# Two blocks with three mixtures of experts on one core: routing of all groups at once, rounding ahead, overflow slots behind the first gathers

## Chip, cores, metric

The kernel runs on one core of one Trainium2 chip. The metric is device microseconds of one execution; lower is better. All data are 32-bit floats. On TensorE "f32" products are full ones; operands named `..._parts` hold values rounded to the short form fp32r, and a high and a low part together stand for the full value.

## What is computed

Two blocks over 256 tokens of width 1,024. The first has two layers (an attention mixer and a MoE each), the second one layer (state-space mixer, attention and a wider MoE). What the change touches is the MoE's choice of experts, the same in all three:

```python
def hier_moe(h, wg, bg, we, be, w_gate, w_up, w_down):
    ...
    gl = (t @ wg + bg).astype(jnp.float32)
    gp = jax.nn.softmax(gl, axis=-1)
    _, gsel = lax.top_k(gl, 1)
    g_oh = jax.nn.one_hot(gsel[:, 0], MOE_GROUPS, dtype=jnp.float32)
    gw = jnp.sum(gp * g_oh, axis=-1, keepdims=True)
    el = (t @ we + be).astype(jnp.float32).reshape(n, MOE_GROUPS, MOE_PER_GROUP)
    el_g = jnp.sum(el * g_oh[:, :, None], axis=1)
    tv, ti = lax.top_k(el_g, MOE_TOPK)
    tw = jax.nn.softmax(tv, axis=-1)
    w_grp = jnp.sum(jax.nn.one_hot(ti, MOE_PER_GROUP, dtype=jnp.float32) * tw[..., None], axis=1)
    comb = ((g_oh * gw)[:, :, None] * w_grp[:, None, :]).reshape(n, MOE_EXPERTS)
    a = jax.nn.silu(jnp.einsum('td,edf->tef', t, w_gate)) * jnp.einsum('td,edf->tef', t, w_up)
    y = jnp.einsum('tef,efd->td', a * comb[:, :, None].astype(a.dtype), w_down)
```

There are 16 experts; the hidden width is 256 in the two MoEs of the first block and 512 in that of the second.

## The kernel before

Everything is written out by hand as one instruction stream per engine, with semaphores. Tokens lie on the 128 partitions in two tiles (`tt` 0 and 1). Weights come through a ring of six slots of 2,048 KB each, filled by SyncE's queue in a fixed order (`PHASES`); the load of tile n waits until `tile_used` says that tile n - 6 has been read. TensorE's stream raises `tile_used` when it has done the last product on a tile.

The three MoEs are called `moe0`, `moe1` (function `small_experts`) and `moe2` (function `wide_experts`). Each is built the same way:

1. The second normalisation's result (`pb`, columns 0 to 1,023) is transposed by TensorE (`token_transposes`, L2164), evacuated with the modulation by ScalarE and VectorE (`trans_out`, L937 and L1303), and multiplied by the router's 20 columns (`thin_products`, L2312; `thin_folded`, L2321). ScalarE also rounds the same rows into high parts (`rounded_pairs`, L994), and GpSimd forms the low parts from them (`low_pairs`, L790).
2. VectorE's `routing` adds the bias (L1481), finds the best group, then that group's best and second expert (`first_of_max` three times, one after the other), and writes `chosen` (L1500). TensorE's `places` (L2335 to L2337) counts the tokens of each expert; VectorE turns that into `place` and into the selection matrices `wide_sel` (L1514), 64 slots for each expert, 8 experts a half.
3. TensorE gathers: `gather(half, c)` multiplies column block c of the rows by the selection (L2375 in the small ones, L2572 in the wide one). `inputs` multiplies the gathered rows by the gate and up weights (L2405, L2627), `down` by the down weights (L2454, L2701), and the result is scattered back.
4. Between the router and the gathers TensorE works on weight tiles of the modulation (`mod_tile`, L2205: four of them in `moe0` and `moe1`, two in `moe2`); ScalarE copies the raw result (L914), and `mod_turn` (L2217) transposes it.

`moe2` has extra slots for experts that more than 64 tokens chose: two experts of each half. VectorE's `more_slots` finds them (L1682 to L1712), writes the selection `more_sel` (L1706, semaphore `more_selected`) and the experts' numbers. GpSimd reads the numbers and copies ("picks", L826) those experts' weights from each pair of ring slots into `picked`; TensorE gathers their rows (`gather_more`, L2582) and multiplies them (L2643). Since the picks read the ring, a pair's slots may be released only after `picked`.

Steps on VectorE that depend on each other are joined by `step`, which waits for the instruction's own semaphore.

## Time and profile before

| what | us |
|---|---|
| three runs | 1330.98, 1336.9, 1338.33 |
| median of them | 1336.9 |
| span of the profiled execution | 1338.1 |

The profiled execution has no time of its own beside its span; the span lies between the second and third of the runs. "Span" is from the first to the last instruction. TensorE is busy 92% of it, the DMA queue of the weights 71.8%, VectorE 33%, ScalarE 20%, GpSimd 9%. In times below, us are counted from the span's start. PEclk is the TensorE clock that was granted, as a share of 2.4 GHz; its lower level is 0.50, 1.2 GHz. The first small MoE runs from about 203 to 341, the second from 565 to 704, the large one from 1058 to 1328.

### The profile page before, as it was taken

What the parts mean: (1) busy time and instruction counts of PE and PEld (TensorE: products, weight loads), DVE (VectorE), ACT (ScalarE), POOL (GpSimd) and SP (SyncE); (2) the same over time, 40 slices, a digit from 0 to 9 for tenths busy, and PEclk for the clock granted to TensorE, in tenths of its full rate; (3) what the DMA queues carried; (4) which work ended last, traced back from release to release, by engine and by line L of the source; (5) the groups of instructions that cost most, each with busy time, mean ns of one, the idle gap of its engine ahead of it and who ended that gap; (6) DMA issues with size and microseconds to landing.
All of it is one profiled execution on the core that took longest, in us unless ns stands there. A gap on an engine that the chain in (4) does not pass through costs nothing.

```text
span 1338.1 us, 17906 instructions
## 1 busy us (share of the span) xinstructions
PE 1237.0 (92%) x7488; PEld 654.8 (49%) x7488; DVE 438.6 (33%) x1143; ACT 265.7 (20%) x622; POOL 115.2 (9%) x202
## 2 busy tenths in 40 slices
PE   4999989999899899999996999999999599999996
PEld 4445745434445665554345855555544443332333
DVE  1102644113313574431144743331123730201133
ACT  0102511121101364111121221113320211120110
POOL 1010010000111000100001000000000222223221
PEclk9899999999899799999997999999999699999999
DMA  9956958999943565399997433294326479999994
GB/s 354 376 171 201 387 213 305 387 387 387 344 144 130 211 230 188 142 364 387 386 387 254 171 126 104 86 382 147 110 85 237 161 290 377 381 378 399 383 384 154
DMA packets 173803, 357.43 MB, mean 267 GB/s; under 512 B 15845, under 2 KB 20502, under 8 KB 173718
## 3 DMA queue, kind: packets, MB, share of 16 engines
q1 hardware_dynamic: 159904, 352.33, 71.8%
q10 hardware_dynamic: 13814, 3.87, 1.3%
q8 instruction: 64, 1.05, 0.3%
q14 instruction: 21, 0.17, 0.0%
HBM read 355.14 MB, written 1.05 MB: 266 GB/s over the span
## 4 chain that ended last, share of the span: by engine, by line
PE 81%; DMA 8%; DVE 5%; ACT 2%; issue 2%; SPq 1%; POOL 0%; DVEq 0%; ACTq 0%
PE bank L2187 19%; PE bank L2627 9%; PE bank L2405 7%; PE bank L2205 5%; PE bank L2923 4%; PE bank L2280 4%; DMA ring<-in_w_down 3%; PE bank L2454 3%; PE bank L2983 3%; DMA ring<-in_moe_w_down 3%; PE bank L2375 3%; PE bank L2701 2%; PE bank L2474 2%; PE bank L2272 2%; DMA ring<-in_ada_w 1%
## 5 line engine op out<-in xcount | busy, mean ns | idle before, releaser
L2187 PE MATMUL bank<-ring,hT 128*128 128x512 f32 x384 | 170.3, 603 | 2.6 <-ACT hT L937 2.4
L2627 PE MATMUL bank<-ring,A 128*64 128x512 f32 x512 | 118.1, 609 | 1.6 <-DVE pb L1784 1.6
L2187 PEld LDWEIGHTS bank<-ring,hT 128*128 128x128 f32 x384 | 73.4, 194 | 91.8 <-issue 91.8
L2405 PE MATMUL bank<-ring,A 128*64 128x512 f32 x512 | 116.0, 598 | 0.0
L2187 PE MATMUL bank<-ring,OT 128*128 128x512 f32 x224 | 97.2, 593 | 1.3 <-ACT OT L1260 0.8
L2205 PE MATMUL bank<-ring,cact 128*32 128x128 f32 x2304 | 84.5, 303 | 9.1 <-DMA ring<-in_ada_w 6.8
L778 POOL TENSOR_TENSOR rstd<-rstd,nhalf 128x1 f32<-128x1 f32 x20 | 15.9, 796 | 797.3 <-DVE rstd L1329 797.3
L2205 PEld LDWEIGHTS bank<-ring,cact 128*32 128x32 f32 x2304 | 70.3, 122 | 22.9 <-issue 15.1
L2627 PEld LDWEIGHTS bank<-ring,A 128*64 128x64 f32 x512 | 35.5, 139 | 74.2 <-issue 73.4
L2187 PEld LDWEIGHTS bank<-ring,OT 128*128 128x128 f32 x224 | 42.2, 190 | 53.5 <-issue 52.5
L2405 PEld LDWEIGHTS bank<-ring,A 128*64 128x64 f32 x512 | 34.2, 136 | 65.3 <-issue 64.2
L2454 PE MATMUL bank<-ring,pb 128*64 128x512 f32 x256 | 57.7, 597 | 2.1 <-DMA ring<-in_moe_w_down 2.1
L2280 PE MATMUL bank<-ring,hT 128*128 128x512 f32 x128 | 55.8, 594 | 0.0
L2923 PE MATMUL bank<-hT,ring 128*128 128x256 f32 x256 | 55.8, 380 | 0.0
L2923 PEld LDWEIGHTS bank<-hT,ring 128*128 128x128 f32 x256 | 48.5, 190 | 6.7 <-issue 0.2
L2983 PE MATMUL bank<-ring,hT 128*128 128x512 f32 x96 | 42.6, 593 | 0.0
L2164 PE MATMUL bank<-ident,pb 128*128 128x128 f32 x128 | 21.7, 331 | 22.0 <-issue 16.4
L2280 PEld LDWEIGHTS bank<-ring,hT 128*128 128x128 f32 x128 | 24.2, 190 | 29.1 <-issue 29.0
L937 ACT ACTIVATE hT<-bank,modc 128x128 f32<-128x128 f32 x48 | 18.0, 459 | 102.8 <-PE bank L2164 101.4
L2454 PEld LDWEIGHTS bank<-ring,pb 128*64 128x64 f32 x256 | 17.6, 136 | 37.4 <-issue 28.5
L567 DVE COPY PT<-bank 128x384 f32<-128x384 f32 (+1 forms) x34 | 17.8, 522 | 52.9 <-PE bank L2297 50.6
L1580 DVE TENSOR_TENSOR A_parts<-bank,OT_parts 128x512 fp32r<-128x512 f32 x32 | 21.6, 690 | 37.9 <-ACT OT_parts L1044 37.8
(491 smaller groups left out, 1701.4 us busy)
## 6 DMA issues: line engine op xcount, KB each, us to landing
...
```

Source lines behind the costliest of these rows:

```text
L2187: ins = mm(B[2 * (m % 2) + tt][:], lhs[:, c, tt * P:(tt + 1) * P], w[:, c, :], start=c == 0, stop=c == C - 1)
L2205: ins = mm(B[MOD_RAW_BANK[G]][32 * q:32 * (q + 1), k * P:(k + 1) * P], cact[:, c0 + c:c0 + c + 1].broadcast_to([P, 32]), w[:, c, q * P:(q ...
L2272: ins = mm(dst, lhs, rhs, start=start, stop=stop)
L2280: ins = mm(B[2 + tt][:], hT[:, c, tt * P:(tt + 1) * P], w[:, c, :], start=c == 0, stop=c == C - 1)
L2375: ins = mm(bank[:], part[:, tt, c * P:(c + 1) * P], wide_sel[:, tt, 512 * half:512 * (half + 1)], start=tt + l == 0, stop=tt + l == 2)
L2405: ins = mm(B[b][64 * odd:64 * (odd + 1), :], wide_h[c][:, slot:slot + 64], w[:, 2 * pair + odd, :, r, :], start=c == 0, stop=c == C - 1)
L2454: ins = mm(B[r][64 * b:64 * (b + 1), :], hidT_small[half][k][:, slot:slot + 64], w[:, 2 * r + b, :], start=k == 0, stop=k == 1)
L2474: ins = mm(B[5 - j + tt][:], wT_small[NR * half + r][:, P * tt:P * (tt + 1)], part[r], start=half + r + l == 0, stop=half == 1 and r + l = ...
L2627: ins = mm(B[b][64 * odd:64 * (odd + 1), :], wide_h[c][:, slot:slot + 64], w[:, 2 * pair + odd, r, :], start=c == 0, stop=c == C - 1)
L2701: ins = mm(B[r][64 * b:64 * (b + 1), :], hidT_wide[half][k][:, slot:slot + 64], w[:, 2 * r + b, :], start=k == 0, stop=k == 3)
L2923: ins = mm(B[2 * (m % 2) + a // 2][:, (a % 2) * T:(a % 2 + 1) * T], w[:, c, a * P:(a + 1) * P], hT[:, c, :], start=c == 0, stop=c == C - 1)
L2983: ins = mm(B[4 + u % 2][:], hT[:, c, (u % 2) * P:(u % 2 + 1) * P], w[:, c, :], start=c == 0, stop=c == C - 1)
```

## The change

1. `routing`: `first_of_max` now works on the group logits and on all four groups' expert logits at once (a tile of 5 x 4 in place of 1 x 4, in the new buffer `rk`). The second `first_of_max` finds each group's second expert. The best group's rows are picked out only at the end, in `chosen` and in the weights. One of three `first_of_max` goes.
2. ScalarE rounds the second token tile (`rounded_pairs(..., 1, ...)`) before it evacuates that tile's transposition, and in `moe2` GpSimd waits for the second normalised tile before it forms the low parts of the first.
3. In the small MoEs `places` stands behind the first modulation tile and the first gather behind the second.
4. In `moe2` the selection of the second half, `select("moe2", 1)`, and the overflow slots (`more_experts`, `more_slots`) are written behind the first gathers' evacuations; TensorE's wait for `more_selected` moves from ahead of all `inputs` to the first `gather_more`.
5. In `moe2`, for the first pair of weight tiles, the wait for `picked` moves behind the main products, and both slots are released together after the overflow products.

```diff
@@ low_pairs (GpSimd) @@
+            if i == 2:
+                pool.wait_ge(s["xn_ready"], MOE["moe2"]["before"] + TT)
             for tt in range(TT):
@@ scalar, for moe0 (the same for moe1 and, with x_high, moe2) @@
         rounded_pairs("moe0", 0, x_high_small)
+        rounded_pairs("moe0", 1, x_high_small)
         trans_out("h1", modulated(0, 3), [1])
         thin_copied("h1")
-        rounded_pairs("moe0", 1, x_high_small)
         pairs_copied("moe0")
@@ vector @@
+        maxima = rk[:].rearrange("p t r e -> p t (r e)")[:, :, 52:61]
+        group_hot, top_hot, second_hot = rk[:, :, 0, :], rk[:, :, 1:5, :], rk[:, :, 9:13, :]
+
+        def select(name, half):
+
+            n, (e0, e1) = MOE[name]["slots"], (8 * half, 8 * half + 8)
+            for tt in range(TT):
+                ins = v.tensor_tensor(wide_sel[:, tt, n * e0:n * e1].rearrange("p (e k) -> p e k", k=n),
+                                      bc(place[:, tt, e0:e1], 2, [P, e1 - e0, n]),
+                                      bc(slot_no[:, 0:n], 1, [P, e1 - e0, n]), ALU.is_equal)
+            ins.then_inc(s["selected"], 1)
...
-            first_of_max(goh, gl, mg, 1)
-
-            prod = rt[:, :, 9:13, :]
-            step(v.tensor_tensor(prod, prod, bc(rt[:, :, 2, :], 3, [P, TT, 4, 4]), ALU.mult))
-            el = rt[:, :, 3:4, :]
-            step(v.tensor_reduce(rt[:, :, 3, :], prod.rearrange("p t g e -> p t e g"), AX.X, ALU.add))
-            first_of_max(rt[:, :, 4:5, :], el, m1, 1)
+            best = rt[:, :, 13:15, :].rearrange("p t r e -> p t (r e)")
+            first_of_max(rk[:, :, 0:5, :], lg, maxima[:, :, 0:5], 5, best[:, :, 0:5])
+            others = rk[:, :, 5:9, :]
             for tt in range(TT):
-                ins = v.scalar_tensor_tensor(rt[:, tt, 6, :], rt[:, tt, 4, :], NEG, rt[:, tt, 3, :], ALU.mult, ALU.add)
+                ins = v.scalar_tensor_tensor(others[:, tt], top_hot[:, tt], NEG, lg[:, tt, 1:5, :], ALU.mult, ALU.add)
             step(ins)
-            first_of_max(rt[:, :, 5:6, :], rt[:, :, 6:7, :], m2, 1)
-            step(v.tensor_tensor(rt[:, :, 6, :], rt[:, :, 4, :], rt[:, :, 5, :], ALU.add))
+            first_of_max(second_hot, others, maxima[:, :, 5:9], 4, best[:, :, 0:4])
+            step(v.tensor_tensor(others, top_hot, second_hot, ALU.add))
...
+            select(name, 0)
             if name == "moe2":
                 return
+            select(name, 1)
@@ wide_experts, vector @@
+            more_experts()
             gathered(0, 1)
             mod_columns(9)
+            more_slots()
             for c in range(1, C, 2):
...
+                if c == 3:
+                    select("moe2", 1)
...
         routing("moe2")
-        more_slots()
         wide_experts(gate2)
@@ small_experts, tensor @@
-            for k in range(3):
+            mod_tile(G, 0)
+            places(i)
+            mod_tile(G, 1)
+            gather(0, 0)
+            for k in range(2, 4):
                 mod_tile(G, k)
-            places(i)
-            mod_tile(G, 3)
-            gather(0, 0)
             mod_turn(G)
@@ wide_experts, tensor @@
-                if c:
+                if c == 0:
+                    pe.wait_ge(s["more_selected"], 2)
+                else:
...
-                if quad:
+                ahead = quad and n > n0 + 1
+                if ahead:
                     pe.wait_ge(s["picked"], (n - n0) // 2 + 1)
...
                 if quad:
+                    if not ahead:
+                        pe.wait_ge(s["picked"], 1)
...
-                    ins.then_inc(tile_used, 1)
+                    ins.then_inc(tile_used, 1 if ahead else 2)
...
-            pe.wait_ge(s["more_selected"], 2)
```

TensorE in `moe0`, from the fold of the router's columns to the first product on expert weights. `cact` is the condition, `Pm` the raw modulation, `pb_parts` the high parts and the selection, `OT_parts` the low parts. Before:

```order
L2205 MATMUL bank<-ring,cact 32x128 x96
L2335 MATMUL bank<-chosen,tri_one 128x32
L2336 MATMUL bank<-chosen,tri_one 128x32
L2337 MATMUL bank<-chosen,tri_one 128x16
L2205 MATMUL bank<-ring,cact 32x128 x32
L2375 MATMUL bank<-pb_parts 128x512
L2375 MATMUL bank<-pb_parts,OT_parts 128x512
L2375 MATMUL bank<-pb_parts 128x512
L2375 MATMUL bank<-pb_parts,OT_parts 128x512
L2217 MATMUL bank<-ident,Pm 128x128 x4
L2375 MATMUL bank<-pb_parts 128x512
L2375 MATMUL bank<-pb_parts,OT_parts 128x512
```

After:

```order
L2220 MATMUL bank<-ring,cact 32x128 x32
L2350 MATMUL bank<-chosen,tri_one 128x32
L2351 MATMUL bank<-chosen,tri_one 128x32
L2352 MATMUL bank<-chosen,tri_one 128x16
L2220 MATMUL bank<-ring,cact 32x128 x32
L2390 MATMUL bank<-pb_parts 128x512
L2390 MATMUL bank<-pb_parts,OT_parts 128x512
L2390 MATMUL bank<-pb_parts 128x512
L2390 MATMUL bank<-pb_parts,OT_parts 128x512
L2220 MATMUL bank<-ring,cact 32x128 x64
L2232 MATMUL bank<-ident,Pm 128x128 x4
L2390 MATMUL bank<-pb_parts 128x512
```

The three counting products moved up by two modulation tiles, and the first gather (four products of 128x512) by two tiles as well; the turn (`ident,Pm`) now follows the last modulation tile directly.

VectorE in `moe2`, from the selection to the second gather's evacuation. `dts` holds the overflow's working values, `cs` a product with `place`, `wr` the modulation columns by pairs, `A` the gathered rows. Before, from the selection on (its four instructions in one row), and the last rows ahead of the evacuation:

```order
L1514 TENSOR_TENSOR pb_parts<-place,slot_no 128x512 x4
L1682 COPY dts<-bank 128x16
L1683 TENSOR_SCALAR dts<-dts 128x16
L1684 MEMSET dts 128x96
L1685 SCALAR_TENSOR_TENSOR dts<-dts,slot_no 128x16
L1686 TENSOR_REDUCE dts<-dts 128x2
L1687 TENSOR_TENSOR dts<-dts 128x2x8
```

```order
L1706 TENSOR_TENSOR pb_parts<-dts,slot_no 128x128 x2
L1709 TENSOR_TENSOR dts<-dts,slot_no 128x64
L1710 TENSOR_REDUCE dts<-dts 128x4
L1711 TENSOR_SCALAR expert_id<-dts 128x2
L1712 TENSOR_SCALAR expert_id<-dts 128x2
L1746 TENSOR_SCALAR A<-bank,wr 128x512
L1353 TENSOR_TENSOR modc<-bank,cols 128x8
L1356 TENSOR_SCALAR modc<-modc 128x8
L1357 MEMSET mark 128x1
```

After (lines of the changed kernel), the selection (two instructions) and then the last rows of `more_experts` and what follows:

```order
L1520 TENSOR_TENSOR place<-bank,chosen 128x32
L1483 TENSOR_TENSOR pb_parts<-place,slot_no 128x512 x2
L1690 COPY dts<-bank 128x16
L1691 TENSOR_SCALAR dts<-dts 128x16
L1692 MEMSET dts 128x96
L1693 SCALAR_TENSOR_TENSOR dts<-dts,slot_no 128x16
L1694 TENSOR_REDUCE dts<-dts 128x2
```

```order
L1702 TENSOR_REDUCE dts<-dts 128x2
L1703 TENSOR_TENSOR dts<-dts 128x2x8
L1758 TENSOR_SCALAR A<-bank,wr 128x512
L1356 TENSOR_TENSOR modc<-bank,cols 128x8
L1359 TENSOR_SCALAR modc<-modc 128x8
L1360 MEMSET mark 128x1
L1709 TENSOR_TENSOR cs<-place,dts 128x64 x2
L1711 TENSOR_REDUCE dts<-cs 128x8
L1712 TENSOR_SCALAR dts<-dts 128x8
L1715 SCALAR_TENSOR_TENSOR dts<-dts 128x2 x2
L1718 TENSOR_TENSOR pb_parts<-dts,slot_no 128x128 x2
L1721 TENSOR_TENSOR dts<-dts,slot_no 128x64
```

The evacuation `A<-bank,wr` and the three rows of the modulation columns behind it moved from behind the last of the overflow's rows into their middle, ahead of the product with `place`.

ScalarE in `moe0`, at the second token tile. `hT` is the transposed and modulated input, `pb_parts` the high parts, `PT` the router's sums. Before:

```order
L994 CAST pb_parts<-pb 128x1024
L937 ACTIVATE hT<-bank,modc 128x128 x4
L908 COPY PT<-bank 128x256
L994 CAST pb_parts<-pb 128x1024
L999 COPY wr<-bank 128x16
```

After:

```order
L997 CAST pb_parts<-pb 128x1024 x2
L940 ACTIVATE hT<-bank,modc 128x128 x4
L911 COPY PT<-bank 128x256
L1002 COPY wr<-bank 128x16
```

The second rounding (`CAST`) moved from behind the copy of the router's sums to ahead of the four activations.

## Rows read from the trace of the kernel before

**Rows 1.** The page: span, and the chain that ended last, by engine.
```profile
span 1338.1 us, 17906 instructions
...
PE 81%; DMA 8%; DVE 5%; ACT 2%; issue 2%; SPq 1%; POOL 0%; DVEq 0%; ACTq 0%
```

**Rows 2.** Windows, `moe0`: busy us by engine, granted clock, DMA share, GB/s.
```profile
235.00:240.00 5.00, 5.00 (x24) 2.44 (x24) 0.81 (x1) 0.78 (x1) 0.00 (x0) 1.00 1.05 387
```

**Rows 3.** Timeline of `moe0`: start, us, engine, line, operation, count, [idle before].
```profile
201.44 1.13 ACT L994 CAST pb_parts<-pb 128x1024 fp32r<-128x1024 f32 x1
...
203.11 6.58 PE L2205 MATMUL bank<-ring,cact 128*32 128x128 f32 x192
...
212.97 0.59 ACT L914 COPY Pm<-bank 128x512 f32<-128x512 f32 x1 [9.57 <-PE bank L2205]
...
213.89 0.60 PE L2217 MATMUL bank<-ident,Pm 128*128 128x128 f32 x4
```

**Rows 4.** Waits of TensorE on weight loads: us in total, times, longest us.
```profile
PE bank L2454 <- DMA ring<-in_moe_w_down: 2.1, 2, 1.5
...
PE bank L2701 <- DMA ring<-in_w_down: 2.7, 4, 1.1
```

**Rows 5.** Timeline of TensorE in `moe2`.
```profile
1051.27 1.97 PE L2164 MATMUL bank<-ident,pb 128*128 128x128 f32 x8 [1.11 <-DVE pb L1337]
...
1058.26 5.62 PE L2205 MATMUL bank<-ring,cact 128*32 128x128 f32 x128
...
1066.33 0.50 PE L2572 MATMUL bank<-pb_parts 128*128 128x512 f32 x1 [1.68 <-DVE pb_parts L1514]
...
1071.87 0.50 PE L2572 MATMUL bank<-pb_parts 128*128 128x512 f32 x1 [3.20 <-DVE pb_parts L1706]
...
1073.39 4.88 PE L2627 MATMUL bank<-ring,A 128*64 128x512 f32 x16
...
1080.16 3.65 PE L2627 MATMUL bank<-ring,A 128*64 128x512 f32 x16
```

**Rows 6.** Timeline of VectorE in `moe2`.
```profile
1042.06 0.81 DVE L1337 TENSOR_SCALAR pb<-x,mv,rstd 128x1024 f32<-128x1024 f32 x1
...
1048.86 2.35 DVE L1337 TENSOR_SCALAR pb<-x,mv,rstd 128x1024 f32<-128x1024 f32 x1
...
1057.41 0.26 DVE L1481 TENSOR_TENSOR rt<-bank,br 128x20 f32<-128x20 f32 x2 [2.77 <-PE bank L2321]
...
1057.91 1.88 DVE L1467 TENSOR_TENSOR rt<-rt 128x8 f32<-128x8 f32 x1
...
1063.36 0.19 DVE L1500 TENSOR_TENSOR chosen<-rt 128x32 f32<-128x32 f32 x1
...
1067.39 0.17 DVE L1682 COPY dts<-bank 128x16 f32<-128x16 f32 x1
...
1070.13 0.36 DVE L1697 TENSOR_TENSOR cs<-place,dts 128x64 f32<-128x64 f32 x2
...
1071.32 0.49 DVE L1706 TENSOR_TENSOR pb_parts<-dts,slot_no 128x128 fp32r<-128x128 f32 x2
```

**Rows 7.** Timeline of GpSimd in `moe2`.
```profile
1048.26 2.40 POOL L790 TENSOR_TENSOR A_parts<-pb,pb_parts 128x1024 fp32r<-128x1024 f32 x1
...
1057.35 2.41 POOL L790 TENSOR_TENSOR A_parts<-pb,pb_parts 128x1024 fp32r<-128x1024 f32 x1 [6.69 <-ACT pb_parts L994]
...
1075.19 0.61 POOL L826 COPY PT<-ring 128x512 f32 x1 [15.43 <-issue]
```

**Rows 8.** Windows, `moe2`: busy us by engine, granted clock, DMA share, GB/s.
```profile
1058.00:1064.00 6.00, 6.00 (x137) 5.51 (x136) 5.25 (x24) 0.22 (x2) 1.77 (x1) 0.65 0.20 37
...
1070.00:1076.00 6.00, 4.13 (x12) 1.58 (x14) 3.25 (x17) 0.78 (x1) 0.81 (x2) 0.72 0.69 278
...
1076.00:1082.00 6.00, 6.00 (x34) 2.94 (x32) 1.95 (x8) 0.46 (x1) 1.48 (x3) 1.00 0.00 0
...
1310.00:1316.00 6.00, 6.00 (x34) 1.76 (x32) 0.00 (x0) 0.00 (x0) 1.17 (x2) 1.00 0.88 328
```

53 lines of the change are left out of this document (27 added, 26 removed).

## Prediction

> **What bounds the kernel now.** I read the page first: the span is 1338.1 us and the chain that ended last is 81% TensorE, 8% DMA and only 5% VectorE [rows 1]. So a cheaper routing on VectorE is worth something only where TensorE waits for it. Next I read the DMA rate in windows. Inside the first small mixture of experts (MoE) the DMA engines are busy all the time and move 387 GB/s [rows 2]. A weight tile of 2,048 KB (2.097 MB) takes 2.097/387 = 5.4 us at that rate. Then TensorE's waits: in the two small MoEs it waits twice for a down-projection tile, 2.1 us in all, the longest 1.5, so the other 0.6; in the large one it waits 2.7 us in four pieces for such tiles [rows 4]. Each small MoE thus has a DMA stream that starts when TensorE releases the first modulation tile (by the code, a tile's load waits for `tile_used`) and does not pause; what TensorE does a little later in front of that wait is swallowed by it. Last I read the timelines around the three routings, where the edits are.
>
> **The small MoEs (moe0; moe1 has the same order).** *Routing.* TensorE does not wait for VectorE here: its three modulation tiles run from 203.11 for 6.58 us [rows 3], and the choice of experts is made beside them. The chain from the sum of logits to `chosen` has 22 waited steps before and 14 after; in the large MoE it reads from 1057.41 to 1063.55, 6.1 us, of which 1.88 - 0.17 = 1.7 us is one stalled comparison [rows 6]. A step costs about 0.2 us, and the new ones (40 elements in place of 8) should cost the same, since the sum over 20 elements twice takes 0.26 us. After: 14 x 0.21 = 3.0 us. The gain is 3.1 us on VectorE, worth nothing here as long as the modulation tiles cover it.
>
> *TensorE's new order.* `places` and the first gather now stand between modulation tiles. The same products run, but the first gather no longer lies between the last modulation tile and `mod_turn`, where it hid ScalarE's copy of the raw modulation (0.59 us, from 212.97; the turn followed at 213.89) [rows 3]. TensorE will stand still for that copy and two handovers: +0.8 us. The slots of the second to fourth modulation tile come free 0.8 to 1.8 us later, but the slot of the first comes free when it did, and one queued tile feeds the DMA engines for 5.4 us, so the stream does not pause. The 0.8 us meets the later wait: hidden in moe0 (1.5 us of wait), all but 0.2 us hidden in moe1 (0.6 us). If that cover were gone it would be +1.6 us.
>
> *Rounding ahead.* ScalarE's second rounding takes 1.13 us and began at 201.44 [rows 3]; now it stands before the four activations that empty the second tile's transposition bank, and they slip by up to about 0.5 us in moe0. The same rows are also waited for from VectorE, which leaves +0.2 us on the path to the router and so on the start of the DMA stream. In moe1 nearly nothing. Bounds 0 and +0.5 for each; I take +0.2 together. What it buys is that GpSimd's second `low_pairs` ends before the routing's first comparison; in moe2 the two began within 0.6 us of each other [rows 6, 7], which is the stall. Sum of both small MoEs: +0.4 us, bounds 0 and +2.6.
>
> **The large MoE (moe2), where the gain is.** Step by step from [rows 5] to [rows 7]:
> 1. GpSimd waits for the second normalised tile before it forms the low parts. Before, its first `low_pairs` (1048.26, 2.40 us) overlapped VectorE's normalisation, which took 2.35 us against 0.81 us for the same form at 1042.06. Now that ends 1.5 us earlier. TensorE had waited 1.11 us for it (transpositions at 1051.27), so the path gains 1.1 us; the other 0.4 us goes to the thin products in front. The Trainium skill, "SBUF — State Buffer", section "Who interferes with whom", says that VectorE and GpSimd share a port pair as an exclusive lock, so that the loser waits for the whole instruction. The two long rows agree; by the rule the reordering would be free of such stalls, as the sum has it.
> 2. Router, modulation tiles (1058.26 for 5.62 us), `places` and the first half of the selection keep their length: `chosen` at about 1059.4 is no longer close to the tiles' end at 1062.8, but it was already covered. So the faster routing is again worth 0, and everything up to the end of `mod_turn` moves by 1.1 us: the first gather from 1066.33 to 1065.2, the turn's end from 1071.87 - 3.20 = 1068.67 to 1067.6.
> 3. The wait of 3.20 us for the overflow slots (`more_selected`) goes. Gather 2 follows at once. It took 1071.87 to 1073.39, 1.5 us; the first two and the short turn took 2.34 us together, so a gather about 1.0 us. Behind the wait the granted clock was the lower of its two levels, 1.2 GHz, for part of the time (0.72 of 2.4 GHz in 1070 to 1076, 1.00 in the next window) [rows 8]. The 16 products of the first weight tile took 4.88 us there against 3.65 us for the next. I take the full clock for both, since the pause that came ahead of the slow rows is gone: first weight tile 1068.6 to 1072.2, second (after the same 1.9 us of gathers) 1074.1 instead of 1080.16. That is 6.1 us: 1.1 + 3.2 + 0.5 + 1.2, rounded.
> 4. What is late next. VectorE: half a selection (1.25 us of 2.50) is left out, so `more_experts` runs from 1067.39 - 1.25 - 1.1 = 1065.0 for 2.7 us (1070.13 - 1067.39). Gather 1's evacuation (0.81 us) ends at 1068.6, and is needed for the second half of the first tile, 1070.4. The modulation columns (0.6 us) and `more_slots` (1070.13 to 1071.81, 1.7 us) end at 1070.9. The overflow gather needs them at 1072.2: 1.3 us to spare. GpSimd began its picks 1075.19 - 1071.81 = 3.4 us after that point, so at 1074.3, and four of 0.61 us end at 1076.7. The changed code waits for them only behind the main products, at 1077.7: 1.0 us to spare. Without that move TensorE would wait 2.6 us.
> 5. DMA. The price of step 4's move is that the first slot is released not by the first product of the second tile but after all of its overflow products, at about 1078.8 (1.0 us for eight, an estimate from the gather's four). Before, it came at 1080.2; only 1.4 us are gained for the first load, about 6 us for the second. The queue was empty then (0 GB/s in 1076 to 1082) and stops at about 1315 (328 GB/s in 1310 to 1316) [rows 8]. The 42 tiles behind the first six need 42 x 5.4 = 228 us; they had 1315 - 1081 = 234, so DMA idled some 6 us in between, mostly in the first pass, where two tiles take TensorE 3.65 x 2 + 1.9 + 2 = 11.2 us and DMA 10.8. That slack lets the loads catch up to TensorE's 6.1 us, nearly. The end of the stage hangs on the last loads [rows 4], so it is their gain that counts: at least 1.4, at most 6.1. I take 5.6, since the later passes leave DMA little idle time to recover the rest.
> 6. The second half of the selection (1.25 us) runs behind the second overflow column block, when VectorE is idle, over 30 us ahead of the gathers that read it: 0. The overlap of GpSimd's picks with `route_weights` may stretch a few VectorE steps; slot sums need them much later: 0.
>
> **Sum.** -5.6 + 0.4 = -5.2 us on the profiled span: 1338.1 to 1332.9. The three runs have their median at 1336.9, 1.2 below the span, so 1331.7 (-0.39%). A change under 0.5% (6.7 us) is about what a measurement of this kernel cannot tell from none.
>
> **Rivals.**
> - *Forecast, 0.58:* 1329.5 to 1333.
> - *DMA takes most of it, 0.20.* If loads in the middle passes run slower than 387 GB/s, or never idle, the later first release rules: gain 1.4 to 3.8, minus 0.4 to 2.6. For it: the small MoEs run at full rate throughout, and the large one nearly does. Against it: 6 us of slack. Time 1334.5.
> - *More is gained, 0.17.* The granted clock was 0.65 in 1058 to 1064, so at 1.2 GHz through most of the two modulation tiles (5.62 us for 128 products, against 6.58 for 192 in moe0) [rows 3, 5, 8]. If less idle time raises it up to 3 us sooner, another 1 to 2 us come, and moe0's and moe1's +0.4 may be 0. With 6.1 from step 3: -8, so 1329. The Trainium skill, "TensorE: Matmul & The Clock Gate", section "The HAM clock gate", says that the slow level is the default and activity lifts it; the slow rows behind the pause agree.
> - *Slower, 0.05.* TensorE's clock falls back in the idle time ahead of the first gather (1.68 us) and stays down through pass 0. Each weight tile then costs up to 3.65 us more; 1.5 tiles eat the gain, and from 3.4 tiles the kernel is slower by over 0.5%. With four, 1331.7 + 14.6 = 1346. Against it: that same idle time did not lower it before.
> - *The change does nothing:* if `more_selected` is as late as TensorE's need by 3 us more than reckoned; it has 1.3 us to spare. Within the second case.
>
> **Range and chances.** The cases from DMA-bound to more gained hold 0.95. Cutting half of each outer tail, and with runs of the kernel before 7 us apart, 1328.3 to 1335.8. Faster by over 0.5% (below 1330.2): 0.17 plus a sixth of the forecast case, 0.27. Slower by over 0.5%: 0.05. Within: 0.68.
>
> **What would show it.** Right: `low_pairs` three times without a long VectorE row beside it; TensorE's wait for `more_selected` gone and the first two weight tiles both at 3.65 us; a pause of 0.7 us before `mod_turn` in moe0 and moe1; the wait for the down tile there shorter by 0.8; the second weight tile of moe2 6 us nearer to the router. Wrong: TensorE waiting for picks or for the overflow slots, more wait for down tiles in moe2 than 2.7 us, or a small MoE that is longer by over 1 us.

## The result, and the profile after

The changed kernel took 1324.12 us, the median of 4 runs (1321.49 to 1324.61), beside 1336.95 us for the kernel before in the same session (4 runs, 1330.98 to 1338.33). The ratio is 0.9913 with a 95% interval of 0.9885 to 0.9941: faster by 12.8 us, where 5.2 were forecast, and below the range of 1328.3 to 1335.8. The profiled execution fell from 1338.1 to 1321.8 us, by 16.3.

The page of the changed kernel: its span, the granted TensorE clock in 40 slices, and the chain that ended last by engine.

```profile
span 1321.8 us, 17890 instructions
...
PEclk8999999999899899999997999999999699999998
...
PE 84%; DVE 5%; DMA 5%; ACT 3%; issue 2%; SPq 1%; POOL 0%; DVEq 0%; ACTq 0%
```

In the chain that ended last TensorE is 84% in place of 81%, and DMA fell from 8% to 5% [rows 1]. Next TensorE's timeline in the large MoE of the changed kernel.

```profile
1034.94 1.33 PE L2179 MATMUL bank<-ident,pb 128*128 128x128 f32 x5 [4.23 <-DVE pb L1340]
...
1042.10 1.97 PE L2179 MATMUL bank<-ident,pb 128*128 128x128 f32 x8
...
1049.09 5.96 PE L2220 MATMUL bank<-ring,cact 128*32 128x128 f32 x128
...
1057.50 0.50 PE L2588 MATMUL bank<-pb_parts 128*128 128x512 f32 x1 [1.68 <-DVE pb_parts L1483]
...
1059.63 0.50 PE L2588 MATMUL bank<-pb_parts 128*128 128x512 f32 x1
...
1060.75 3.65 PE L2646 MATMUL bank<-ring,A 128*64 128x512 f32 x16
1064.34 0.33 PE L2600 MATMUL bank<-pb_parts 128*128 128x128 f32 x1
...
1066.30 3.65 PE L2646 MATMUL bank<-ring,A 128*64 128x512 f32 x16
1069.88 0.62 PE L2664 MATMUL bank<-PT,cols 128*32 128x512 f32 x1
```

The waits of 1.11 us ahead of the second row and of 3.20 us ahead of the second gather (now at 1059.63) [rows 5] are gone, and both weight tiles take 3.65 us. From the first row, the transposition with which the part begins, to the second weight tile it took 31.4 us. In the kernel before that transposition stands here:

```profile
1042.92 1.97 PE L2164 MATMUL bank<-ident,pb 128*128 128x128 f32 x8 [3.88 <-DVE pb L1337]
```

So before it took 1080.16 - 1042.92 = 37.2 us. VectorE's timeline of the changed kernel beside it:

```profile
1040.88 0.80 DVE L1340 TENSOR_SCALAR pb<-x,mv,rstd 128x1024 f32<-128x1024 f32 x1
...
1048.55 0.20 DVE L1469 TENSOR_REDUCE rk<-rt 128x10 f32<-128x40 f32 x1
1048.78 0.20 DVE L1470 TENSOR_TENSOR rk<-rt,rk 128x40 f32<-128x40 f32 x1
...
1051.35 0.19 DVE L1506 TENSOR_TENSOR chosen<-rk 128x32 f32<-128x32 f32 x1
...
1062.42 0.49 DVE L1718 TENSOR_TENSOR pb_parts<-dts,slot_no 128x128 fp32r<-128x128 f32 x2
```

And GpSimd's:

```profile
1041.76 4.77 POOL L793 TENSOR_TENSOR A_parts<-pb,pb_parts 128x1024 fp32r<-128x1024 f32 x2 [1.45 <-DVE pb L1340]
1066.30 0.61 POOL L829 COPY PT<-ring 128x512 f32 x1 [19.76 <-issue]
1066.85 1.17 POOL L829 COPY tmp<-ring 128x512 f32 x2
1067.96 0.61 POOL L829 COPY gate<-ring 128x512 f32 x1
```

The normalisation takes 0.80 us, no step of the choice is stalled, and GpSimd has done both low parts (1041.76 + 4.77 = 1046.5) before the choice starts at 1048.55. The overflow slots are ready at 1062.9, 1.4 us ahead of the gather that wants them at 1064.34. The picks end at 1068.6 and are wanted at 1069.88. In `moe0` the timeline shows the new order's two small waits:

```profile
202.44 1.95 PE L2220 MATMUL bank<-ring,cact 128*32 128x128 f32 x64
205.33 0.41 PE L2350 MATMUL bank<-chosen,tri_one 128*128 128x32 f32 x2 [0.93 <-DVE chosen L1506]
...
214.31 0.55 PE L2232 MATMUL bank<-ident,Pm 128*128 128x128 f32 x3 [0.68 <-ACT Pm L917]
```

And TensorE's waits in total, in answer to [rows 4]:

```profile
PE bank L2722 <- DMA ring<-in_w_down: 2.1, 3, 0.8
PE bank L2232 <- ACT Pm L917: 2.0, 3, 0.7
PE bank L2350 <- DVE chosen L1506: 1.9, 2, 0.9
```

The waits for the small MoEs' down tiles are no longer there. Those of the large one add up to 2.1 us, less than before, so its loads kept pace. Yet the large MoE gives only 8.3 of the 16.3 us: 5.9 up to the second weight tile and 2.4 from there to the end. More than 5 us of the profiled gain lie between 410 and 460, where no instruction differs. Windows of the kernel before and then of the changed one (busy us by engine, granted clock, DMA share, GB/s):

```profile
410.00:460.00 50.00, 45.09 (x345) 31.15 (x345) 20.42 (x59) 12.67 (x32) 3.24 (x7) 0.80 0.48 173
1095.00:1130.00 35.00, 34.45 (x178) 13.58 (x177) 3.56 (x9) 5.89 (x9) 7.42 (x13) 0.95 0.99 385
```

```profile
410.00:460.00 50.00, 43.81 (x430) 29.94 (x428) 24.23 (x77) 17.31 (x50) 2.35 (x5) 0.93 0.53 187
1095.00:1130.00 35.00, 34.45 (x178) 13.77 (x176) 4.05 (x9) 6.21 (x9) 7.78 (x14) 1.00 1.03 409
```

In the first the granted clock is 0.80 against 0.93 (1.00 is 2.4 GHz, 0.50 the lower level of 1.2 GHz), so 50 x 0.20 / 0.5 = 20 us of it ran at the lower level before and 7 after. The second window is in `moe2`, and will matter below. Either the changed code keeps TensorE's clock up, or the clock differs by chance from one execution to the next. The experiments are about this and about what each part is worth.

### The profile page after: what moved, and what is told of

The parts are those of the page before. It is cut to its first block, busy times and chain, and to the rows that moved or that the text cites. A ratio compares the mean times of both kernels' runs of the same rounds, so it can differ in the third digit from the quotient of the medians.

```text
span 1321.8 us, 17890 instructions
## 1 busy us (share of the span) xinstructions
PE 1222.3 (92%) x7488; PEld 645.3 (49%) x7488; DVE 430.5 (33%) x1128; ACT 265.5 (20%) x622; POOL 114.9 (9%) x202
## 4 chain that ended last, share of the span: by engine, by line
PE 84%; DVE 5%; DMA 5%; ACT 3%; issue 2%; SPq 1%; POOL 0%; DVEq 0%; ACTq 0%
PE bank L2202 19%; PE bank L2420 9%; PE bank L2646 9%; PE bank L2469 4%; PE bank L2943 4%; PE bank L2295 4%; PE bank L2220 4%; DMA ring<-in_w_down 3%; PE bank L3003 3%; PE bank L2390 3%; PE bank L2722 2%; PE bank L2489 2%; PE bank L2287 2%; PE bank L2312 1%; DMA ring<-in_ada_w 1%
## 5 line engine op out<-in xcount | busy, mean ns | idle before, releaser
L2646 PE MATMUL bank<-ring,A 128*64 128x512 f32 x512 | 115.2, 597 | 1.7 <-DVE pb L1800 1.7
L2420 PE MATMUL bank<-ring,A 128*64 128x512 f32 x512 | 116.0, 598 | 0.0
L2220 PE MATMUL bank<-ring,cact 128*32 128x128 f32 x2304 | 80.8, 293 | 10.6 <-DMA ring<-in_ada_w 7.6
L2220 PEld LDWEIGHTS bank<-ring,cact 128*32 128x32 f32 x2304 | 66.7, 118 | 24.4 <-issue 17.0
L2469 PEld LDWEIGHTS bank<-ring,pb 128*64 128x64 f32 x256 | 17.8, 136 | 34.6 <-issue 29.6
## 6 DMA issues: line engine op xcount, KB each, us to landing
ring<-in_w_down SPq DMA_DIRECT2D x16, 2048.0 KB, 19.9
```

The costliest lines, as they stand in the source:

```text
L2220: ins = mm(B[MOD_RAW_BANK[G]][32 * q:32 * (q + 1), k * P:(k + 1) * P], cact[:, c0 + c:c0 + c + 1].broadcast_to([P, 32]), w[:, c, q * P:(q ...
L2420: ins = mm(B[b][64 * odd:64 * (odd + 1), :], wide_h[c][:, slot:slot + 64], w[:, 2 * pair + odd, :, r, :], start=c == 0, stop=c == C - 1)
L2469: ins = mm(B[r][64 * b:64 * (b + 1), :], hidT_small[half][k][:, slot:slot + 64], w[:, 2 * r + b, :], start=k == 0, stop=k == 1)
L2646: ins = mm(B[b][64 * odd:64 * (odd + 1), :], wide_h[c][:, slot:slot + 64], w[:, 2 * pair + odd, r, :], start=c == 0, stop=c == C - 1)
```

## The experiments

In the 18 runs "before" is the kernel before, timed on the same chip beside each group: 1337.28 us (median of 23 runs), 1337.53 (29) and 1337.56 (18) for the three timed groups. The runs of one kernel scatter widely, those of the kernel before from 1326.7 to 1340.7, so I read the traces of all executions by stage. The table gives the time between the starts of the same two TensorE products in each trace, and in brackets how many of these us the granted clock was at the lower level. The stages are `moe0` (from 196 to the first down product, 302 in the profile of before), the code from 411 to 455, `moe1` (555 to 665), `moe2`'s beginning (1042.92 to the second weight tile, 1080.16), its next 50 us, and the rest. Left out are the start (its end lies at 192.8 to 196.2), 302 to 411 (108.4 to 109.8 us in all), 455 to 555 (99.6 to 101.0) and 665 to 1043 (377.8 to 380.8).

```
               moe0          411-455      moe1          moe2 begin   next 50      rest     span
before         106.3 ( 3.4)  43.9 (20.5)  109.8 ( 6.8)  37.2 (22.7)  49.8 (3.4)   208.1   1338.1
before_a       104.9 ( 0.0)  43.9 (20.5)  109.6 ( 6.8)  37.4 (23.0)  49.8 (3.4)   207.4   1335.2
before_b       104.9 ( 0.0)  37.8 ( 6.8)  107.5 ( 0.0)  37.5 (19.9)  49.8 (3.4)   208.5   1328.7
before_c       107.3 ( 6.8)  39.2 ( 9.8)  108.9 ( 3.4)  36.1 (20.3)  48.1 (0.0)   208.1   1330.9
after          105.5 ( 0.0)  37.8 ( 6.8)  108.3 ( 0.0)  31.4 (18.8)  48.1 (0.0)   207.4   1321.8
again          105.5 ( 0.0)  37.8 ( 6.8)  108.5 ( 0.0)  31.3 (18.7)  48.1 (0.0)   207.5   1321.5
again_2        105.7 ( 0.0)  37.8 ( 6.8)  108.9 ( 3.4)  29.6 ( 9.6)  48.1 (0.0)   207.2   1321.8
again_3        108.4 (10.2)  41.0 (13.7)  111.1 (10.2)  31.0 (17.1)  48.1 (0.0)   208.3   1331.6
again_4        108.4 (10.2)  42.2 (17.0)  109.2 ( 3.4)  29.5 (12.7)  48.1 (0.0)   208.0   1328.9
wide           106.4 ( 3.4)  43.9 (20.5)  109.8 ( 6.8)  32.2 (19.3)  48.1 (0.0)   208.3   1332.1
round          107.2 ( 6.8)  37.8 ( 6.8)  108.8 ( 3.4)  36.3 (22.1)  49.8 (3.4)   207.4   1330.8
round_2        105.1 ( 0.0)  43.9 (20.5)  109.2 ( 3.4)  34.6 (13.0)  49.8 (3.4)   207.3   1332.7
route_order    108.9 (10.2)  41.0 (13.7)  111.4 (10.2)  37.3 (22.8)  49.8 (3.4)   208.2   1341.6
wide_round     107.3 ( 6.8)  39.2 ( 9.9)  109.3 ( 3.4)  29.5 (12.9)  48.1 (0.0)   207.3   1324.0
no_order       105.1 ( 0.0)  43.9 (20.5)  109.7 ( 6.8)  29.5 (12.5)  48.1 (0.0)   207.4   1324.1
old_routing    108.4 (10.2)  41.0 (13.7)  110.1 ( 3.4)  29.5 (12.9)  48.1 (0.0)   207.7   1328.4
no_late_pick   108.4 (10.2)  41.0 (13.7)  109.1 ( 3.4)  31.9 (12.7)  51.5 (6.8)   207.6   1333.9
late_pick_2    105.7 ( 0.0)  37.8 ( 6.8)  109.1 ( 3.4)  31.9 (12.7)  51.5 (6.8)   207.4   1327.5
warm_before    106.0 ( 0.0)  39.1 ( 9.7)  109.0 ( 0.0)  34.6 (10.2)  49.8 (3.4)   207.8   1329.6
warm_after     106.4 ( 0.0)  37.8 ( 6.8)  109.5 ( 0.0)  28.6 ( 3.4)  48.1 (0.0)   208.5   1322.1
```

Two things stand out. The stage from 411 to 455 takes 37.8 to 43.9 us whatever the kernel, and always the same for the same us at the lower clock: (43.9 - 37.8) / (20.5 - 6.8) = 0.44 us for each. The two stages of `moe2` follow the code.

**The changed kernel again (again).** No edit.

> The changed kernel, unchanged, timed in more rounds. Two theories of the 12.8 us by which the median fell where 5.2 were forecast. CLOCK BY CHANCE: some 6 us come from the large MoE's start, as forecast, and the rest is TensorE's granted clock, which happened to be at its lower level more often in the profiled execution of before (at the routers of both small MoEs, at the compression stage before the second attention, in the large MoE's first pass) in stretches where both kernels do the same. Then over many runs the ratio moves towards 0.995, and the mean granted clock of single runs scatters by as much as it differs between the kernels. CLOCK BY THE CODE: the edits at the routers keep the clock at its upper level. Then the ratio stays at 0.991, and the mean clock of every run of this kernel is above that of every run of before.

1324.05 us (4 runs, 1324.0 to 1325.6), ratio 0.9908, interval 0.9892 to 0.9924, mean clocks 0.974 to 0.975 against 0.959 to 0.973 in the 23 runs of before. I took this for the theory of the code. It was too early, as again_3 and again_4 show.

**Parts alone.** The wide part (wide): the overflow slots and the second half of the selection behind the gathers, and the later wait for picks.

```diff
+            more_experts()
             gathered(0, 1)
             mod_columns(9)
+            more_slots()
...
-            pe.wait_ge(s["more_selected"], 2)
...
-                if quad:
+                ahead = quad and n > n0 + 1
+                if ahead:
                     pe.wait_ge(s["picked"], (n - n0) // 2 + 1)
```

> The kernel before with parts 4 and 5 alone (overflow slots and second half of the selection behind the first gathers, the first pair's picks waited for late). The waited 3.2 us and the slow products behind it should go. By the chance theory this part is worth 4 to 5 us (ratio 0.9965 to 0.997) whatever the small MoEs do. By the code theory it is worth the same, and the missing 7 us must show up in the other parts.

1330.84 us (6 runs, 1325.9 to 1334.1), ratio 0.9943, interval 0.9925 to 0.9961: -6.4. The table shows it without the clock's scatter, since all other stages are those of before to 0.2 us: `moe2`'s beginning -5.0 (37.2 to 32.2), where step 3 of the prediction has 4.9, and the next 50 us -1.7, which the prediction does not have.

The rounding (round): the second rounding ahead of the activations in all three MoEs, and GpSimd's wait for the second normalised tile.

```diff
+            if i == 2:
+                pool.wait_ge(s["xn_ready"], MOE["moe2"]["before"] + TT)
...
         rounded_pairs("moe2", 0, x_high)
+        rounded_pairs("moe2", 1, x_high)
         trans_out("h5", modulated(2, 3), [1])
         thin_copied("h5")
-        rounded_pairs("moe2", 1, x_high)
```

> The kernel before with part 2 alone (rows rounded ahead in all three MoEs, GpSimd's wait in the large one). Forecast step: 1.1 us at the large MoE's second token tile, +0.2 at the first small one, and 1.7 to 2.2 us less on VectorE's routing that TensorE does not wait for: ratio 0.999. By the code theory with the rounding as its cause: 0.995, with the clock at its upper level at both small routers.

1333.12 us (12 runs, 1325.7 to 1335.6), ratio 0.9964, interval 0.9944 to 0.9983: -4.2. The forecast of 0.999 lies outside the interval. In `moe2` the two profiles have 36.3 and 34.6 in place of 36.1 to 37.5 us, so 1.6 us in the mean belong to that stage; what the rest of the 4.2 is, the two profiles don't show.

Routing and order (route_order): the shorter choice and the new place of `places` and the first gather in the small MoEs, without the rounding.

```diff
-            for k in range(3):
-                mod_tile(G, k)
+            mod_tile(G, 0)
             places(i)
-            mod_tile(G, 3)
-            gather(0, 0)
+            mod_tile(G, 1)
+            gather(0, 0)
+            for k in range(2, 4):
+                mod_tile(G, k)
```

> The kernel before with parts 1 and 3 alone (all groups' best experts at once; counting products and first gather between the modulation tiles). Forecast step: 0 to +0.4 us, ratio 1.000, and TensorE stands 0.7 us ahead of the turn. By the code theory with the order as its cause: ratio 0.995 to 0.997.

1340.77 us (12 runs, 1336.8 to 1343.6), ratio 1.0028, interval 1.0011 to 1.0044: slower by 3.5 us, where 0 to 0.4 were forecast. VectorE's timeline of this kernel in `moe0` shows a part of the reason.

```profile
202.91 2.30 DVE L1468 TENSOR_TENSOR rk<-rt,rk 128x40 f32<-128x40 f32 x1
205.24 0.20 DVE L1469 TENSOR_TENSOR rk<-rk,first 128x40 f32<-128x40 f32 x1
...
207.58 0.19 DVE L1495 TENSOR_TENSOR chosen<-rk 128x32 f32<-128x32 f32 x1
```

The stalled comparison (2.30 us in place of 0.20, beside GpSimd's low parts, which run from 202.74 for 2.41 us) eats two thirds of the 3.1 us that the choice got shorter, and TensorE now wants `chosen` behind one tile, not three: its timeline shows a wait though the lower clock stretched that tile.

```profile
207.83 0.64 PE L2337 MATMUL bank<-chosen,tri_one 128*128 128x32 f32 x2 [0.96 <-DVE chosen L1495]
```

What this costs can be read beside again_3, the changed kernel with the same us at the lower clock in both small MoEs and no wait for `chosen` in either: 108.9 against 108.4 us in `moe0` and 111.4 against 111.1 in `moe1`. That is 0.8 us for the stall. The new order's own waits cost 0.9 to 1.6 us (see the small MoEs below), and what is left of the 3.5 us the stages don't show.

The three parts give -6.4 - 4.2 + 3.5 = -7.1 alone, and -13 together. The stall, which the rounding removes, is some 0.8 us of the difference; that the rest is the clock's scatter is likely and not shown.

**One part undone.** No_order puts TensorE's order in the small MoEs back (the diff above reversed, on the changed kernel).

> The changed kernel with TensorE's order in the two small MoEs put back as before (three modulation tiles, places, the fourth, the first gather, the turn); everything else as changed. By itself the new order cost 3 us, because the stalled comparison made TensorE wait for the chosen experts. THEORY ORDER COSTS EVEN WITH ROUNDING AHEAD: the changed kernel waits 0.93 us for the chosen experts and 0.68 us for the raw modulation's copy in moe0; both waits go, and the time falls by 0 to 1.5 us, to 1322.5 to 1324 (ratio to before 0.989 to 0.990). THEORY THE PARTS ADD UP: without the new order what is left is the sum of the wide part alone (-6.1 us) and the rounding alone (-4.2 us), so about 1326.5 to 1327 (ratio 0.992), and the low-clock stretch in moe0 near 202 is back, since TensorE runs 192 products there at once while it was at the lower level. The profile decides: granted clock in 198 to 210 and in 420 to 456.

1328.7 us (12 runs, 1319.3 to 1333.8), ratio 0.9938, interval 0.9914 to 0.9962. The time is nearer to the second theory's, but not for its reason: the profile has no low clock in `moe0`, which takes 105.1 us, 0.4 below the changed kernel's at the same clock. Its runs reach from as low as the changed kernel's to 1333.8, and the profiled one had 20.5 us at the lower clock in 411 to 455.

No_late_pick waits for GpSimd's picks ahead of the first overflow tile's main products again, and again releases that tile's slot at its first product (a part of the edit):

```diff
-                ahead = quad and n > n0 + 1
-                if ahead:
+                if quad:
                     pe.wait_ge(s["picked"], (n - n0) // 2 + 1)
...
-                    ins.then_inc(tile_used, 1 if ahead else 2)
+                    ins.then_inc(tile_used, 1)
```

> The changed kernel, but TensorE again waits for GpSimd's picks ahead of the main products of the first overflow tile, and releases that tile's slot at its first product. In the changed kernel's trace that tile's main products begin at 1066.30 and the last pick ends at 1068.6. THEORY TENSORE'S PATH SETS THE END: TensorE waits 2.3 us more at that tile, and the kernel is slower than the changed one by 2.3 us, to 1326.3 (ratio to before 0.992). THEORY DMA SETS THE END (the loads behind the first slots run without a pause): the first slots are released at 1068.7 in place of 1070.9, so the first load of the stream starts 2.2 us sooner, and the kernel is not slower, down to 1322. Prediction's step 5 took a gain between the two; in between: half of each, the same time within 1 us.

1332.92 us (12 runs, 1327.6 to 1340.1), ratio 0.9969, interval 0.9946 to 0.9992. Late_pick_2 is the same kernel, run beside the changed one (again_2).

> The kernel of no_late_pick once more. Its one added wait measured 2.34 us, but its median was 8.9 us above the changed kernel's. THEORY CHANCE: the rest, 6.6 us, was clock by chance, and beside the changed kernel it is now 2 to 4 us slower than that, wherever the two lie. THEORY THE CODE: it is again 7 to 9 us slower, at 1332 to 1334.

> The changed kernel once more, unchanged, beside the kernel of no_late_pick. No_late_pick has the changed kernel's instructions in the same order up to 1066 us, yet its profiled execution was already 6.4 us late at 1053, all of it at the lower clock (10.2 us of it at 202, 13.7 at 441), and its 12 runs scatter from 1327.6 to 1340.1. So the clock differs between executions of the same instructions. THEORY CHANCE (where in the program the level changes falls by chance in each execution): the eight tight runs of the changed kernel so far (1321.5 to 1325.6) were a lucky draw; further runs scatter up to 1330 and over, the median is 1326 to 1330, ratio to before 0.992 to 0.995. THEORY THE CODE: the runs stay within 1321 to 1326 and the ratio at 0.991.

Late_pick_2 took 1332.07 us (12 runs, 1325.9 to 1338.6), ratio 0.9958, interval 0.9937 to 0.9979; again_2 1324.12 (6 runs, 1318.8 to 1333.3), ratio 0.9911, interval 0.9876 to 0.9946. The two profiles agree to 0.2 us in every stage up to `moe2`, so they show the undone part alone. TensorE's timeline and then two windows of late_pick_2:

```profile
1068.54 1.04 PE L2645 MATMUL bank<-ring,A 128*64 128x512 f32 x3 [2.36 <-POOL gate L829]
...
1102.12 0.33 PE L2600 MATMUL bank<-pb_parts 128*128 128x128 f32 x1 [0.55 <-ACT w2c L1080]
```

```profile
1066.00:1072.00 6.00, 3.64 (x14) 1.51 (x15) 5.37 (x25) 0.00 (x0) 2.28 (x4) 0.82 0.21 40
...
1116.00:1122.00 6.00, 6.00 (x28) 2.40 (x26) 0.53 (x1) 0.78 (x1) 2.28 (x4) 0.87 0.99 370
```

The wait is 2.36 us. Behind it, and again some 45 us later, TensorE runs at the lower clock for a while (0.82 and 0.87), where again_2 has no low clock: +2.3 (31.9 against 29.6), +3.4 (51.5 against 48.1), 5.7 in the span. So here a wait of 2.4 us cost more than twice itself, and the earlier release of the slot gave nothing of it back. The medians differ by 8 us; the 2.3 us above 5.7 are within the scatter.

**Extra work to keep the clock up.** Products of zeros that nobody reads, in TensorE's waits around the three routers; warm_before on the kernel before, warm_after on the changed one.

```diff
+        def filler(n):
+            for _ in range(n):
+                mm(B[7][:], zeros[:], bc(ident[:], 1, [P, 4, P]), start=True, stop=True)
...
         mod_turn(8)
+        filler(7)
         token_transposes("h5", xn, "xn_ready", 10, tiles=[0])
+        filler(5)
         pe.wait_ge(s["mod_ready"], 9)
         thin_products(wr[2], 20, "h5", (0,))
         token_transposes("h5", xn, "xn_ready", 10, tiles=[1])
+        filler(3)
```

> The kernel before, with nothing of the change, and extra work: products of zeros that nobody reads, put where TensorE waits around the three routers (3 products of 512 columns in moe0 and in moe1 ahead of the router's products; 7, 5 and 3 around the transpositions of moe2's normalised rows). They cost up to 1.6 us of TensorE's time at the full clock where they are longer than the wait, twice that at the lower. THEORY THE CLOCK FOLLOWS TENSORE'S IDLE TIME AT THE ROUTERS: the low-clock stretches behind the three routers (3.4 to 20 us long in the kernel before) shrink, mean clock rises from 0.965 to 0.972 or more, and the time falls by 2 to 6 us though work was added: 1331 to 1335. THEORY THE CLOCK COMES FROM ELSEWHERE: low stretches stay as they are, and the time is the same or up to 1.6 us longer: 1337 to 1339.

> The changed kernel with the same extra products at the same places. THEORY THE CLOCK FOLLOWS TENSORE'S IDLE TIME AT THE ROUTERS: the stretch from 1032 to 1052 (20 us at the lower clock in the changed kernel) shrinks and the time falls by 1 to 4 us, to 1320 to 1323. THEORY THE CLOCK COMES FROM ELSEWHERE: 1324 to 1326. In both kernels together: if the changed kernel gains nothing from the extra products and the kernel before does, the change had already removed that idle time.

Warm_before: 1331.96 us (12 runs, 1330.4 to 1339.3), ratio 0.9982, interval 0.9960 to 1.0003. Warm_after: 1326.26 (6 runs, 1324.4 to 1328.0), ratio 0.9926, interval 0.9903 to 0.9949. Mean clocks rose to 0.972 to 0.980 and 0.979 to 0.984. In `moe2`'s beginning the us at the lower clock fell from 19.9 to 23.0 in the four profiles of before to 10.2, and from 9.6 to 18.8 in the five of the changed kernel to 3.4; the stage took 34.6 us against 37.1 in the mean, and 28.6 against 30.5. So with less idle time of TensorE the clock is at its lower level for less time there. But without low clock on either side `moe0` got 1.1 and 0.9 us longer, `moe1` 1.5 and 1.1, and the stage ahead of `moe2`, in which seven of the products stand, 1.3 and 1.9 (379.8 against 378.5, 380.8 against 378.9). The products cost about what they gave. The changed kernel is not faster for them. Warm_before's median fell by 5.6 us while the interval of its ratio reaches 1: no gain is shown.

**Old routing.** Wide_round has the rounding and the wide part alone; old_routing is the changed kernel with the old choice of 22 steps.

```diff
-            first_of_max(rk[:, :, 0:5, :], lg, maxima[:, :, 0:5], 5, best[:, :, 0:5])
+            first_of_max(goh, gl, mg, 1)
...
+            first_of_max(rt[:, :, 4:5, :], el, m1, 1)
...
-            first_of_max(second_hot, others, maxima[:, :, 5:9], 4, best[:, :, 0:4])
+            first_of_max(rt[:, :, 5:6, :], rt[:, :, 6:7, :], m2, 1)
```

> Rounding ahead, the overflow slots moved and the later picks, but the old routing and the old order of TensorE in the small MoEs: the kernel of no_order without the faster routing. PREDICTION'S STEP 2 (the faster routing is worth nothing where TensorE has three modulation tiles to do beside it): the same time as no_order within 2 us, so 1327 to 1330 (ratio 0.992 to 0.995). RIVAL (the choice of experts is late after all, in one of the three): slower than no_order by 1 to 3 us in each MoE where it is, 1331 or more, and the trace has TensorE waiting for the chosen experts.

> The changed kernel with the old routing chain (22 waited steps in place of 14), TensorE's new order kept. In the changed kernel TensorE waits 0.93 us for the chosen experts in moe0, behind one modulation tile. THEORY THE FASTER ROUTING IS WHAT PAYS FOR THE NEW ORDER: eight steps of 0.23 us more make that wait 1.8 us longer in each small MoE; in moe0 the wait for the down tile (1.5 us) no longer hides it all. Slower than the changed kernel by 2 to 4 us, at 1326 to 1328 if that is at 1324. RIVAL (the DMA stream sets the small MoEs' end, and it starts with the first tile's release all the same): within 1 us of the changed kernel.

Wide_round: 1326.29 us (6 runs, 1322.1 to 1328.9), ratio 0.9910, interval 0.9889 to 0.9930. Old_routing: 1330.75 (7 runs, 1328.7 to 1334.2), ratio 0.9952, interval 0.9934 to 0.9969. The first is 2.4 us below no_order, which has the faster routing, and neither trace has TensorE waiting for `chosen`: no gain of the routing is seen with the old order. In the second, `moe0` takes 108.4 us as in again_3 and again_4 at the same clock, `moe1` 110.1 against again_4's 109.2, and the span is 0.5 us below again_4's. So by the stages the old routing costs 0 to 1 us, in executions in which the lower clock stretches the one tile that covers the choice; there is no profile of it with the full clock in `moe0`. Its median says 6.6 above again_2's. Medians a few us apart can't carry such a question here.

**Chance or code.** More profiles of unchanged kernels, before_a, before_b and before_c of the kernel before, again_3 and again_4 of the changed one, and round_2.

> The kernel before, unchanged, for a second profiled execution of it. The lower clock in 420 to 456 (20.5 us of it in the first profile, 6.8 us in three profiles of the changed kernel, where the code is the same) is where 5.5 us of the profiled gain came from. THEORY CHANCE: other executions of the kernel before show it shorter too, down to 6.8 us, with the span shorter by half of the difference. THEORY THE CODE: it stays at 17 us or more in each.

> The kernel before, a third profiled execution. The same two theories as for before_a. Two stretches that should be there in each execution, because TensorE stands still ahead of them: the one behind the 3.2 us wait in moe2 (at 1072.5 in the first profile), and none of 6.8 us or more shorter than 17 us only if the code decides in 420 to 456.

> The kernel before, a fourth profiled execution. The same two theories as for before_a; four executions together say how often 420 to 456 runs 17 us or more at the lower clock.

> The kernel of round (the rounding ahead alone) once more, for a second profiled execution. In the first, 420 to 456 had 6.8 us at the lower clock, and its 12 runs scatter from 1325.7 to 1335.6. THEORY CHANCE: another length now, or the same with another span. THEORY THE CODE: again 6.8 us. In both: the stretches behind the 3.2 us wait of moe2 (1066) and near 1117, each 3.4 us, are there again, since the wait is.

> The changed kernel, a fourth profiled execution (the first three all have one stretch of 6.8 us at the lower clock near 439, and spans of 1321.5 to 1321.8). The four executions of the kernel before have 20.5, 20.5, 6.8 and 10.2 us there. THEORY CHANCE WITH THE SAME ODDS: executions of the changed kernel with 10 to 20 us there exist too, with spans up to 1329. THEORY THE CODE MAKES THEM RARE: again 6.8 us and 1321 to 1323.

> The changed kernel, a fifth profiled execution, with the same two theories as again_3. Of either, the wait of TensorE for overflow slots is gone, and with it the low stretches behind it and near 1110 to 1124 that all executions with that wait or with a wait for picks have.

The window of 410 to 460 in before_b, and then in again_3:

```profile
410.00:460.00 50.00, 43.90 (x447) 29.99 (x447) 24.00 (x82) 17.32 (x50) 2.36 (x5) 0.93 0.54 188
```

```profile
410.00:460.00 50.00, 45.15 (x354) 30.86 (x352) 23.00 (x63) 13.07 (x34) 5.88 (x10) 0.86 0.55 191
```

Before_b runs it at 0.93, like the first profiles of the changed kernel, and its span is 1328.7 us, 9.4 below the first profile of the same kernel. Again_3 runs it at 0.86 and took 1331.6 us, again_4 1328.9. Round_2 has 20.5 us at the lower clock where round had 6.8. So the 6.1 us of that stretch (43.9 against 37.8) come about with no change of code. The runs of again_3 and again_4 were 1334.1 and 1331.3 us; those of before_a, before_b and before_c 1337.2, 1330.6 and 1332.8.

## Why the prediction was wrong

**In short.** The step that failed is the one from the profile to a time and a range: the prediction took the granted clock outside `moe2` as one profile showed it, put no term for it in the sum, and took a range of 7.5 us. The runs showed 9.4 and 10.1 us between profiles of one kernel. The steps inside `moe2` came out nearly as forecast, but for a second stretch of low clock (1.7 us) that the sum does not have.

**What the code is worth.** I compare two executions whose clock agrees up to `moe2`, before_b and again_2: 1328.7 to 1321.8, -6.9 us. By the means of the table, over four executions of the kernel before and five of the changed one: `moe2`'s beginning 37.1 to 30.5, -6.5; the next 50 us 49.4 to 48.1, -1.3. In the small MoEs only executions with the same us at the lower clock compare: `moe0` without low clock 104.9 to 105.6, +0.7; `moe1` +0.9 without low clock, +0.2 with 3.4 us of it. Together -6.5 - 1.3 + 0.7 + 0.5 = -6.6 (0.5 stands between 0.9 and 0.2). The sum forecast -5.2.

**What was measured, and what stays open.** All 16 runs of the changed kernel (four groups) lie from 1318.8 to 1334.1, mean 1325.8; the 79 of the kernel before from 1326.7 to 1340.7, mean 1336.6. That is -10.8, with 2.2 as the uncertainty of the first mean (twice its standard deviation of 4.44 over the root of 16), if the runs are independent. The ends of both ranges differ by 7.9 and 6.6 us, which is near the code's own part; the medians by 13, because most runs of the changed kernel lie near the lower end of its range and most of the kernel before near the upper end of its own. The first eight runs of the changed kernel all fell between 1321.5 and 1325.6, the last eight have a mean of 1327.5, so luck in the first is likely.

The mean granted clock of each run, on record for these 16 and for 75 of the 79, gives a second estimate: a straight line through time and clock with a step between the kernels has the step at -5.9 us (± 1.3) at equal clock, and the other 4.9 us of the 10.8 go with a clock of 0.974 in place of 0.967. Some of that clock is the change's own, the 8.6 us less at the lower level in `moe2`'s beginning and the next 50 us (24.0 to 15.4 in the mean).

Whether the code also changes the clock ahead of `moe2` the profiles don't settle, but they give no sign of a gain. `moe2` begins at 1038.7 us in the mean of the four profiles of before and at 1038.8 in that of the five of the changed kernel; the whole difference of their spans, 8.1 us, lies behind it. Over the nine profiles with the new order of TensorE in the small MoEs and the nine without (those with extra products left aside) it begins at 1040.3 and 1039.4, with 3.7 as the uncertainty of the difference. The stages are not independent draws either. With the new order `moe0` has no low clock and 411 to 455 has 6.8 us of it (four profiles), or they have 10.2 and 13.7 to 17.0 (five). Without it `moe0` has 0 to 6.8, and 411 to 455 has 20.5 in five of nine, which the new order never has. So the new order may shift the odds in both places, one way in `moe0` and the other in 411 to 455; seen after the fact in eighteen profiles, this is not shown.

**By the prediction's steps.**
- *Step 1* (-1.1, the normalisation without GpSimd beside it): right. The transpositions start 1.19 us nearer to the stage's beginning, the row is 0.80 us. The Trainium skill, "SBUF — State Buffer", section "Who interferes with whom", has this as an exclusive lock; the trace agrees, in `moe2` and in route_order's 2.30 us row, which ends at 205.21, just behind GpSimd's at 205.15: one waiting instruction, while the next step takes 0.20 us again.
- *Step 2* (the faster routing worth 0): right for `moe2` and, with the rounding ahead, for the old order (wide_round against no_order; 29.5 us for both in `moe2`). Its reading that TensorE does not wait for VectorE in the small MoEs came from a profile in which the lower clock stretched the three tiles to 6.58 us. In before_b they took 5.45 us and TensorE waited 0.71 us for `chosen` in each small MoE; in before_a it did so in `moe0`. With the rounding ahead the wait is gone at full clock too, with the old choice of 22 steps (round_2, 5.45 us).
- *Step 3* (-3.2 wait, -0.5 and -1.2 clock): right: with step 1, -5.9 at the second weight tile in the first profile and -6.5 in the mean, against -6.1. *What failed is that the step ended there*, the one term that the sum for `moe2` lacks. It counted the lower clock behind the wait only at the two tiles next to it. A second low stretch about 50 us behind goes with it: 1.7 us (3.4 us at the lower clock in "next 50") in 7 of the 8 profiles with the wait for overflow slots, 6.8 us at the lower clock in the two with the wait for picks, none in the ten with neither.
- *Step 4*: right. Slots ready 1.4 us early against 1.3, picks 1.3 against 1.0, and 2.36 us of wait without the move against 2.6. The cost of that wait is 5.7, since it brings the clock down too.
- *Step 5* (DMA keeps 0.5 of the 6.1 us): nothing was kept. From the second weight tile to the end before takes 257.9 us, after 255.5, of which 1.7 us is the low stretch. The lower bound of 1.4 was never in question, and the value of 5.6 was too low: the 5.9 to 6.5 us reached the end whole.
- *The small MoEs* (+0.4): nearly. The turn's wait is 0.68 us, and the down tile's wait is gone. Not foreseen was a wait of 0.93 us for `chosen` in each: I priced the steps of the choice nearly right (14 in 3.3 us against 3.0), but looked for its cover in three modulation tiles, and the new order leaves one. Where the lower clock stretches that tile, as in again_3 and again_4, the wait is not there. At the same clock the two cost 0.7 and 0.2 to 0.9 us.

**The step that failed by most** is the one not written down: the granted clock outside `moe2` was taken as it stood in one profile, as a term of nothing without a reason, and the range from three runs 7 us apart. The profiled execution of the kernel before, 1338.1, was the longest of four, and these differ by 9.4 us with no instruction changed. The rival "more is gained" named the clock but looked for it in `moe2` and priced it at 2 us. By stages the change gives 1 to 2 us more than forecast; the rest of the miss, some 6 us of the median, goes with the clock. Whether by chance alone stays open, as said above. The Trainium skill, "TensorE: Matmul & The Clock Gate", section "The HAM clock gate", says that what watches TensorE's activity is free-running and does not start anew with a kernel, so that the number of slow products differs between runs of one kernel; the profiles of unchanged kernels agree, with 6.8 to 20.5 us at the lower clock in 411 to 455, 9.4 us between spans of the kernel before and 10.1 between those of the changed one.

No version clearly beats the changed kernel. Wide_round, without the faster routing and the new order, is within 2.2 us of it, which these scatters don't separate: by medians and by stages the gain comes from the rounding, the late overflow slots and the late wait for picks.
